# The retention output projection of a two-layer block: seven Strassen products in place of full-depth products

## What is computed

```python
att = sliding_window_attention(aq, ak, av, att_sinks)
ret = retention_chunkwise(rq, rk, rv)
ret = head_group_norm(ret, ret_gn_gain) * jax.nn.silu(rg)
merged = jax.nn.sigmoid(ga) * (att @ w_att_o) + jax.nn.sigmoid(gr) * (ret @ w_ret_o)
x = x + merged @ w_out
```

## Time and profile before

| | |
|---|---|
| runs | 2552.01, 2551.42, 2550.05 us (median 2551.42) |
| profiled execution | 2549.01 us, of which the span from first to last instruction is 2547.2 us |
| DVE busy | 1555.7 us, 61% |
| ACT busy | 1032.7 us, 41% |
| POOL busy | 1210.2 us, 48% |
| DMA | 46.3% of the 16 engines' span |

### The profile page before, as it was taken

How to read it: one execution, slowest core, us unless ns; L and a number is a source line. 1 busy time by engine, 2 the same in 40 slices (tenths; PEclk the granted TensorE clock), 3 DMA queues, 4 the chain that set the end, 5 groups by cost and what they waited for, 6 DMA issues and landing times. The chain is left out here.

```text
span 2547.2 us, 34818 instructions
## 1 busy us (share of the span) xinstructions
PE 2518.6 (99%) x12750; PEld 2100.7 (82%) x12750; DVE 1555.7 (61%) x2576; ACT 1032.7 (41%) x2097; POOL 1210.2 (48%) x970
## 2 busy tenths in 40 slices
PE   8999999999999999999999999999999999999998
PEld 7888888777888988888888878898889888888887
DVE  6455444675436545454599852248657666587789
ACT  5332333584224322232444552147646233254443
POOL 4587766354525767676212672314556444200205
PEclk9999999999999999999999999999999999999999
DMA  6565665705551233333753345548443333364434
GB/s 220 203 238 208 226 229 190 281 18 190 191 189 67 96 137 114 117 117 108 273 191 102 100 151 164 175 93 180 143 125 116 108 110 118 135 233 143 177 100 169
DMA packets 171158, 397.55 MB, mean 156 GB/s; under 512 B 22818, under 2 KB 43938, under 8 KB 167330
## 3 DMA queue, kind: packets, MB, share of 16 engines
q1 hardware_dynamic: 170988, 395.32, 46.3%
HBM read 282.69 MB, written 112.31 MB: 155 GB/s over the span
## 5 line engine op out<-in xcount | busy, mean ns | idle before, releaser
L2450 POOL TENSOR_TENSOR WL<-WRAW,WH 128x512 fp32r<-128x512 f32 (+1 forms) x150 | 250.1, 1668 | 360.3 <-ACT WH L1126 359.9
L876 PE MATMUL PS<-HH,WL 128*128 128x512 f32 (+1 forms) x976 | 367.6, 377 | 1.0 <-DVE HS L2016 1.0
L879 PE MATMUL PS<-HH,WH 128*128 128x512 f32 (+1 forms) x976 | 366.5, 375 | 0.0
L878 PE MATMUL PS<-HL,WH 128*128 128x512 f32 (+1 forms) x976 | 366.5, 375 | 0.0
L1652 DVE TENSOR_TENSOR WL<-TS,WH 128x512 fp32r<-128x512 f32 x228 | 230.5, 1016 | 174.3 <-ACT WH L1126 174.1
L944 PE MATMUL PS<-WH,DAL 128*128 128x512 f32 x756 | 294.7, 390 | 0.4 <-DVE WL L1959 0.4
L946 PE MATMUL PS<-WH,DAH 128*128 128x512 f32 x756 | 294.4, 389 | 0.0
L945 PE MATMUL PS<-WL,DAH 128*128 128x512 f32 x756 | 294.4, 389 | 0.0
L2642 POOL TENSOR_TENSOR X<-X,DV 128x512 f32<-128x512 f32 x56 | 90.9, 1646 | 349.2 <-DVE DV L2079 270.9
L876 PEld LDWEIGHTS PS<-HH,WL 128*128 128x128 f32 x976 | 183.8, 188 | 34.3 <-DVE HS L2016 1.3
L1126 ACT ACTIVATE WH<-TS 128x512 fp32r<-128x512 f32 x228 | 138.4, 621 | 180.6 <-POOL TS L2466 180.5
(11 more groups left out here) (359 smaller groups left out, 5880.1 us busy)
## 6 DMA issues: line engine op xcount, KB each, us to landing
WRAW<-in_u_f SPq DMA_DIRECT2D x56, 512.0 KB, 3.7
WRAW<-in_u_in SPq DMA_DIRECT2D x54, 512.0 KB, 4.1
WRAW<-scr_t SPq DMA_DIRECT2D x52, 512.0 KB, 3.7
scr_h<-HS SPq DMA_DIRECT2D x96, 256.0 KB, 2.3
WRAW<-in_u_gu SPq DMA_DIRECT2D x44, 512.0 KB, 3.6
scr_t<-TTa SPq DMA_DIRECT2D x19, 1024.0 KB, 4.8
WRAW<-in_u_out SPq DMA_DIRECT2D x24, 512.0 KB, 3.6
scr_x<-X SPq DMA_DIRECT2D x24, 512.0 KB, 5.0
```

The source lines that it names most:

```text
L876: e.matmul(PS[:, b, 0:wd], wl[:, blk(kk)], op_moving(q, kk, c0, wd, 0), start=(kk == 0), stop=False)
L878: e.matmul(PS[:, b, 0:wd], wh[:, blk(kk)], op_moving(q, kk, c0, wd, 1), start=False, stop=False)
L879: mm = e.matmul(PS[:, b, 0:wd], wh[:, blk(kk)], op_moving(q, kk, c0, wd, 0), start=False, stop=(kk == 3))
L2450: e.tensor_tensor(lo, raw, hi.bitcast(F32), ALU.subtract).then_inc(*c.inc("w_lo_p", i))
```

## The change

The retention's output projection becomes seven products P1, P2, P5, P6, P3, P7, P4 (in that order, `DORDER`), each of four groups m = 0 to 3 of 12 matmuls: 28 groups, 336 matmuls in place of 384. P2 is accumulated on the banks of P1, P3 on those of P5, P4 on those of P7, after ACT (P1, P5) or DVE (P7) has copied or drained them. "U" is P1+P6, "11" is P1+P2, "22" is first P5, then P5+U. The 16 merges go with the groups of P6, P3, P7 and P4; each has now three DVE operations: one with a bank as an operand (P6: U plus the bank; P3, P4: bank plus U; P7: bank plus "22"), then the multiplication by one gate and the addition of the other with both operands in SBUF. DVE makes the operand sums S1, S3, S2, S4 of the gated retention result (16 operations) and the low halves of S1 and S2, POOL the low halves of S4 and S3 and the four sums "22"+U; the low halves of A21 are not made any more. The weights come as 28 halves of 128x512, low halves alternately on DVE (`r0`) and POOL (`r1`), in place of eight whole units; four of the seven are sums that POOL makes ahead of time, so `NPAIR` goes from 27 to 31, and ten pairs in place of six are done in the first FFN, at m = 2, 4, ..., 20. The gate multiplications of the retention result go with the attention outputs as `GATE_AO` says, sixteen with ten, none after. The first group of the product with `w_out` waits for merge 7 (tile 7 of the first half), the second for merge 15 (tile 6 of the second half), which is the last.

```diff
-NPAIR = 27
+NPAIR = 31
...
-    units("u_ro", range(8))
+    for p in DORDER:
+        for m in (0, 2):
+            for x in range(2):
+                ROP[p, m + x] = len(ops)
+                ops.append((f"r{x}", len(order), n_pos()))
+            order.append(("r", (DPROD[p][1], m)))
...
-    LATE = [("P1", 1, 3 * g, 0) for g in range(1, 7)], [("P5", 1, 3 * g, 0) for g in range(1, 7)], [("P1", 1, 3 * g + 1, 0) for g in range(1, 7)]
-    N_RV, N_LATE = 3, 6
+    LATE = [[(p, 1, m + x, 0) for m in range(2, 22, 2)] for p, x in (("P1", 0), ("P5", 0), ("P1", 1))]
+    N_RV, N_LATE = 3, 10
...
     def t_weights(g):
-        return WU["u_dn"][2 * g:2 * g + 2] if g < FF1 // 2 else WU["u_f2"][2 * g - FF1:2 * g - FF1 + 2]
+        for name, t0 in (("u_f2", PAIRS_OF[2]), ("u_ro", T_RO), ("u_dn", 0)):
+            if g >= t0:
+                return WU[name][2 * (g - t0):2 * (g - t0) + 2]
...
-        return kind in ("B11", "B21") or i == PAIR[2, 0] + 6
+        return kind in ("B11", "B21", "r1") or i == PAIR[2, 0] + 6
...
-    RO2 = [(n, half) for half in range(2) for n in range(6)] + [(n, half) for half in range(2) for n in range(6, 8)]
+    GATE_AO = {1: 6, 3: 7, 4: 8, 6: 9, 7: 10, 9: 11, 11: 12, 12: 13, 14: 14, 15: 15}
+    RO_ON = {"P2": "P1", "P3": "P5", "P4": "P7"}
+    MERGED = ([(2 * m, 0) for m in range(4)] + [(2 * m + 1, 0) for m in range(4)]
+              + [(2 * m + 1, 1) for m in range(4)] + [(2 * m, 1) for m in range(4)])
+    MERGE_AT = ["P6", "P3", "P7", "P4"]
...
-        for n, half in RO2:
-            proj_t(("ro2", n, half), U["u_ro", n], half, RH, RL, low="rg_l")
+        for p in DORDER:
+            q = DPROD[p][0]
+            for m in range(4):
+                key, i, onto = ("roP", p, m), ROP[p, m], p in RO_ON
+                if onto:
+                    b = bk.again(key, ("roP", RO_ON[p], m))
+                    w.wait_ge(*bk.empty(key))
+                else:
+                    b = open_bank(key, p in RO_ON.values())
+                w.wait_ge(*lo_done(i))
+                wh, wl, hi, lo = half_slot(WH, i), half_slot(WL, i), ro_half(q, RH), ro_half(q, RL)
+                for kk in range(4):
+                    w.wait_ge(*ro_low(q, kk))
...
+                mm.then_inc(*bk.fill(key))
+                used(i, key)
+            for m in range(4 if p in RO_ON else 0):
+                bk.drop(("roP", p, m))
...
-            w.wait_ge(*c.at("mg_l", (7, tt // 4)))
+            w.wait_ge(*c.at("mg_l", (6 if tt // 4 else 7, tt // 4)))
...
+            if j >= 4 or half == 0:
+                w.wait_ge(*c.at("rg_m", i))
+                e.activation(RH[:, j, hs(half)], QK[:, j, hs(half)], ACT.Copy).then_inc(*c.inc("rg_h", (j, half)))
+            if i in GATE_AO:
+                feed(("ao", *AOG[GATE_AO[i]]))
...
+        for p in DORDER:
+            for m in range(4):
+                key = "roP", p, m
+                if p in ("P1", "P2", "P5"):
+                    w.wait_ge(*bk.full(key))
+                    e.activation(ro_sum({"P1": "U", "P2": "11", "P5": "22"}[p], m), PS[:, bk.at(key), :],
+                                 ACT.Copy).then_inc(*bk.free(key))
+                if p in ("P2", "P5", "P6"):
+                    ro_high({"P2": "S2", "P5": "S4", "P6": "S3"}[p], m)
+                if p in MERGE_AT:
+                    i = 4 * MERGE_AT.index(p) + m
+                    n, half = MERGED[i]
+                    w.wait_ge(*c.at("mg_a", i))
+                    if p == "P6":
+                        w.wait_ge(*ro_low("S2", 3))
+                        w.wait_ge(*ro_low("S4", 3))
+                    if p == "P3":
+                        w.wait_ge(*ro_low("S3", 3))
+                    e.activation(HH[:, n, hs(half)], MR[:, i % 2, :], ACT.Copy).then_inc(*c.inc("mg_h", (n, half)))
+                feed(key)
...
-            if i + N_TAIL < 16:
-                att_out(i + N_TAIL)
-                feed(("ao", *AOG[i + N_TAIL]))
-        for i, (n, half) in enumerate(RO2):
-            key = "ro2", n, half
-            w.wait_ge(*bk.full(key))
+            if i in GATE_AO:
+                att_out(GATE_AO[i])
+                feed(("ao", *AOG[GATE_AO[i]]))
...
+        def ro_sums(q, j):
+            left, right, sign = {"S1": ("A21", "A22", ALU.add), "S3": ("A11", "A21", ALU.subtract),
+                                 "S2": ("S1", "A11", ALU.subtract), "S4": ("A12", "S2", ALU.subtract)}[q]
+            if q == "S1":
...
+            e.tensor_tensor(ro_whole(q)[:, j, :], ro_whole(left)[:, j, :], ro_whole(right)[:, j, :], sign).then_inc(
+                *c.inc("s_ov", ("ro", q, j)))
...
+        def ro_lows(q, j):
+            w.wait_ge(*c.at("h_hi", ("ro", q, j)))
+            e.tensor_tensor(ro_half(q, RL)[:, j, :], ro_whole(q)[:, j, :], ro_half(q, RH)[:, j, :].bitcast(F32),
...
+        def merge(i):
+            n, half = MERGED[i]
+            p, m, mr = MERGE_AT[i // 4], i % 4, MR[:, i % 2, :]
+            key = "roP", p, m
+            if i >= 2:
+                w.wait_ge(*c.at("mg_l", MERGED[i - 2]))
+            if p == "P6":
...
+            elif p == "P7":
+                src = ro_sum("22", m)
+                w.wait_ge(*bk.full(key))
+                w.wait_ge(*c.at("s_op", ("ro", "22", m)))
+                e.tensor_tensor(src, PS[:, bk.at(key), :], src, ALU.add).then_inc(*bk.free(key))
+                w.wait_ge(*bk.out(key))
+            else:
+                src = mr
+                w.wait_ge(*bk.full(key))
+                w.wait_ge(*bk.out(("roP", "P6", m)))
+                e.tensor_tensor(mr, PS[:, bk.at(key), :], ro_sum("U", m), ALU.add).then_inc(*bk.free(key))
+                w.wait_ge(*bk.out(key))
             w.wait_ge(*c.at(f"lg{i % 2}", i))
             w.wait_ge(*c.at(f"lm{i % 2}", i))
-            if i >= 2:
-                w.wait_ge(*c.at("mg_l", RO2[i - 2]))
-            e.tensor_tensor(MR[:, i % 2, :], PS[:, bk.at(key), :], MG[:, i % 2, 0, :],
-                            ALU.mult).then_inc(*bk.free(key))
-            w.wait_ge(*bk.out(key))
-            e.tensor_tensor(MR[:, i % 2, :], MR[:, i % 2, :], MG[:, i % 2, 1, :],
-                            ALU.add).then_inc(*c.inc("mg_a", i))
-            feed(key)
+            e.tensor_tensor(mr, src, MG[:, i % 2, 0, :], ALU.mult).then_inc(*c.inc("s_ov", ("ro", "mg", i)))
+            w.wait_ge(*c.at("s_ov", ("ro", "mg", i)))
+            e.tensor_tensor(mr, mr, MG[:, i % 2, 1, :], ALU.add).then_inc(*c.inc("mg_a", i))
+
...
+        for j in range(4):
+            ro_sums("S1", j)
+        for p in DORDER:
+            for m in range(4):
+                key = "roP", p, m
+                if p == "P1":
+                    ro_lows("S1", m)
+                    ro_sums("S3", m)
+                    ro_sums("S2", m)
+                elif p == "P2":
+                    ro_lows("S2", m)
+                    ro_sums("S4", m)
+                elif p == "P6":
+                    w.wait_ge(*bk.full(key))
+                    w.wait_ge(*bk.out(("roP", "P1", m)))
+                    e.tensor_tensor(ro_sum("U", m), PS[:, bk.at(key), :], ro_sum("U", m), ALU.add).then_inc(*bk.free(key))
+                if p in MERGE_AT:
+                    merge(4 * MERGE_AT.index(p) + m)
+                feed(key)
...
+        def merged_low(i):
+            n, half = MERGED[i]
+            w.wait_ge(*c.at("mg_h", (n, half)))
+            e.tensor_tensor(HL[:, n, hs(half)], MR[:, i % 2, :], HH[:, n, hs(half)].bitcast(F32),
+                            ALU.subtract).then_inc(*c.inc("mg_l", (n, half)))
+
         for i in range(16):
             j, half = GATED[i]
+            if j < 4 and half:
+                if i in GATE_AO:
+                    feed(("ao", *AOG[GATE_AO[i]]))
+                continue
...
+        for p in DORDER:
+            for m in range(4):
+                key = "roP", p, m
+                if p in ("P5", "P6"):
+                    q = "S4" if p == "P5" else "S3"
+                    w.wait_ge(*c.at("h_hi", ("ro", q, m)))
+                    e.tensor_tensor(ro_half(q, RL)[:, m, :], ro_whole(q)[:, m, :], ro_half(q, RH)[:, m, :].bitcast(F32),
+                                    ALU.subtract).then_inc(*c.inc("s_op", ("ro", "lo", q, m)))
+                if p == "P3":
+                    w.wait_ge(*bk.out(("roP", "P5", m)))
+                    w.wait_ge(*bk.out(("roP", "P6", m)))
+                    e.tensor_tensor(ro_sum("22", m), ro_sum("22", m), ro_sum("U", m),
+                                    ALU.add).then_inc(*c.inc("s_op", ("ro", "22", m)))
+                if p in MERGE_AT:
+                    merged_low(4 * MERGE_AT.index(p) + m)
+                feed(key)
...
+            if name == "r":
+                kind, m = i
+                if kind[0] == "T":
+                    for t in range(T_RO + m, T_RO + m + 2):
+                        w.wait_ge(*c.at(f"ts{t_set(t)}", ("out", t)))
+                    src = bass.AP(scr_t.tensor, scr_t.offset + 2048 * P * (T_RO + m) + 512 * T_SLOT[kind],
```

(15 more changed lines are left out.)

## The result

| | before | after |
|---|---|---|
| median | 2551.51 us | 2581.39 us |
| lowest to highest of 4 runs | 2550.05 to 2552.01 | 2579.80 to 2582.28 |
| span of the profiled execution | 2547.2 us | 2578.9 us |

The ratio is 1.0117, with a 95% interval of 1.0100 to 1.0135: slower, as forecast, but 18.4 us beyond the 2563.0 forecast and outside of the range (2546 to 2569).

What follows compares the result with a forecast made beforehand. PE was taken to bound the kernel. Later start of w_out's second group +9.0, before P6 +1.0 and slow matmuls +1.6 gave +11.6 us on 2551.4: 2563.0 us, range 2546 to 2569.

Steps and rivals of the forecast that it cites:

- Matmuls removed: Retention's output projection on PE: 48 fewer matmuls at 0.2267 us save 10.9 us, before anything is given back.
- The walk: DVE's merges from P6 to P4 take 63.95 us, so w_out's second group starts 9.0 us later than now.
- DVE keeps pace: Rival, in the merges: POOL's and DVE's SBUF operations hardly meet, 8.4 us gained, 2543.0 us; chance 0.16.
- each waits for the whole of the other's operation: Rival, in DVE-POOL meetings: 0.24 us more in some 25 of them, 6 us, 2569 us; chance 0.10.
- the two share without gaps: Rival, in the merges: DVE and POOL work totals 56.1 us, 0.2 us gained, 2551.2 us; chance 0.15.
- Before P6: Gates to S2's low halves: the last low half of S1 comes 1 us late at P5, shifting the walk +1.0 us.
- PE after idle time: After 11.7 us idle before w_out's second group, eight matmuls take 0.2 us more each: +1.6 us, bounds 0 and 3.
- Weight sums: First FFN: four more pairs, 22 us of operations, fit in POOL's 119 us of idle time, so 0.
- My rival for it: Rival, in the first FFN: weight sums make POOL late with low halves, at most 5 us, 2568 us; chance 0.04.

Runs made afterwards that it cites:

- e4: Kernel before with only the sixteen gate multiplications interleaved with the ten attention outputs: 2550.0 us, ratio 1.0002.
- e13: e5 with sums S3 and S4 on 8 columns and RG loads cut to 32 of 512 columns from the fifth on: 2569.6 us, ratio 1.0080.
- e5: e1 plus DVE making all four low halves of S1 before adding S3, and of S2 before S4: 2576.8 us, ratio 1.0107.
- e1: Changed kernel with ACT copying P1's four banks to U between gate tiles 12 to 15: 2575.6 us, ratio 1.0106.
- e8: Kernel before with four added, unread weight-sum pairs, ten in the first FFN at m = 2, 4, ..., 20: 2553.9 us, ratio 1.0015.
- e9: e8 with the first FFN's ten pairs at m = 1, 3, ..., 19 instead: 2550.2 us, ratio 1.0001.
- e2: Changed kernel with each merge's multiplication and addition reading the bank, not their SBUF operand, sums left out: 2569.2 us, ratio 1.0080.
- e10: e5 with ACT's and w_out's orders changed, "11" merged from banks, "22" by DVE, S3/S4 by POOL, last weight pair as in e9: 2564.4 us, 1.0056.

## Why the prediction was wrong, step by step

**Matmuls removed, -10.9: right.** 12702 in place of 12750, and the spacing of the new products' matmuls is 0.2267 wherever PE has not stood.

**The walk, 63.95 us: right.** 66.2 measured. The mean of the 32 SBUF operations is (8.6 + 8.3 + 23.7) / 32 = 1.27 us, 1.26 in the walk. The units' waits for ACT are 4.9 us in three, 1.65 each in the walk. The last low half came 2.0 us behind DVE, 2.05 forecast. Of the 2.2 us too little, the waits for MG (3.0) make the most; I had taken 0 and bounded them by 2. The rival "DVE keeps pace" (a mean under 0.98) is refuted by these rows, and so are "each waits for the whole of the other's operation" (6 us more over 32 operations, a mean of 1.45) and "the two share without gaps" (56.1 us; POOL was idle for 18.9 us of 682 to 749).

**Before P6, +1.0: this step failed.** The chain started at 682.4, which is 11.7 us after the 670.7 that the forecast comes to. Two faults lie beside each other, and each alone makes the chain late:
- I followed the operands of P2 but not its bank. "The matmuls of P1 and P2 use tiles gated long before" is true; that P2 also waits for ACT's copy of P1, and what stands ahead of that copy in ACT's order, I did not write down. It made a stop of 9.4 us and 2.5 us of slow matmuls. The bound of 4 us for the early part knew of S1's low halves alone.
- I had DVE ready for its first merge step when PE had done P6's first group, and it was not. The gates end at 647.6 and not 642.6, though interleaved (e4: 648.4 without the rest of the change; e13: the loads of RG are 3.7 us of it). The last low half of S2 then came 25.0 us later, at 672.6, where I had allowed 25.9. Behind it stood one more sum and two weight halves, up to 680.0. My account before P6 has DVE's 24 sums and low halves and POOL's weight halves, but none of the weight halves that DVE makes itself. There were seven: 7.5 us and 4.3 us of waiting for ACT's high halves in the changed kernel, 10.1 us and 0.6 in e5. In all the front work took 32.4 us (32.3 in e5, 31.3 in e1).

DVE's weight halves in 648 to 680 us of the changed kernel, then the end of its front work:

```profile
L1735 DVE TENSOR_TENSOR WL<-WRAW,WH 128x512 fp32r<-128x512 f32 x7 | 7.5, 1072 | 4.3 <-ACT WH L1181 4.3
...
670.81 1.77 DVE L1999 TENSOR_TENSOR RL<-QK,RH 128x512 fp32r<-128x512 f32 x1
672.51 0.68 DVE L1994 TENSOR_TENSOR QK<-QK 128x512 f32<-128x512 f32 x1
673.16 1.73 DVE L1735 TENSOR_TENSOR WL<-WRAW,WH 128x512 fp32r<-128x512 f32 x1
678.60 1.36 DVE L1735 TENSOR_TENSOR WL<-WRAW,WH 128x512 fp32r<-128x512 f32 x1 [3.71 <-ACT WH L1181]
```

The last wait of 3.71 us may itself come from PE's stop (ACT's high half stands there behind copies of P5's banks), but in e1 and e5, without the stop, DVE is no earlier than 678.9 and 681.1. So e1, which undoes only the first fault, gained some 3 us by the ratios.

**PE after idle time, +1.6: mechanism right, too small.** I costed the slow matmuls of one stop. There were four stops in this stretch and one in the down projection, with 2.5 + 1.7 + 1.7 + 2.6 + 1.6 = 10.1 us of slow matmuls. The stops at P7 and P4 cost nothing more, as I had written, and their slow matmuls neither, since the last merge was later still. The 2.5 us behind the stop at P2 are in the late start of the chain; the 2.6 us behind the last stop and the 1.6 us in the down projection count in full. The stop ahead of w_out itself was 9.4 us, "some 10" in the forecast. That the granted clock reads 1.00 at the kernel's start does not stand in the earlier trace rows, which begin at 607 us; that row is in the last section.

The Trainium skill (TensorE: Matmul & The Clock Gate, Wait — 56ns, not 53.3ns?) gives 426.7 ns from start to start for 512 columns at 1.2 GHz. The 0.43 us in the timeline agree.

**Weight sums, 0: failed.** They cost 3.9 us by e8 (3.7 between e8 and e9), and the changed kernel shows a stop of the same kind (2.2 us at 1281.7, 0.4 before). I had weighed POOL's and PE's time and taken the change of steps for a gain. What counted was that the last of ten pairs now ends at m = 20, so that its store falls into a stretch in which the DMA engines are busy for 0.92 to 0.96 of the time. My rival for it had POOL's work as its mechanism, which e9 refutes.

**The sum again**, by what was measured at each place, against the 2563.0:

| step | forecast | measured | difference |
|---|---|---|---|
| start of the chain | 670.7 | 682.4 | +11.7 |
| length of the chain | 63.95 | 66.2 | +2.2 |
| low half behind it | 2.05 | 2.0 | 0 |
| slow matmuls at w_out | 1.6 | 2.6 | +1.0 |
| weight sums | 0 | 3.7 to 3.9 | +3.8 |
| sum | | | +18.7 |

The median is 18.4 us above the forecast. By the spans (31.7 us apart, where the medians are 29.9) 1.4 us more would have to be found. Counted from the end, the same matmul of PE lies 29.9 us later than before at 1712 us and 31.7 later from 1957 us on; the cause of that step is open.

## What to carry to other kernels

When a product is accumulated on a bank that another engine must read first, follow that reader in its own written order, as one follows operands; and when one late thing is found, ask who else would have been late at the same place, because taking it away gains only the difference (9.4 us of stop, some 3 us of time here).

When the time is counted that an engine needs ahead of a step, its part of the weight work belongs in the list: seven weight halves were missing here, 8 to 12 us with their waits.

Where both queues are full, each SBUF operation of POOL costs DVE 1.1 us (128x512), so POOL is no place to move DVE's SBUF work to; the operations that escape are those with an operand in PSUM (0.69 us beside a POOL that is busy for three quarters of the time in e2, 1.27 with both operands in SBUF). Hidden work has to be hidden on every resource: look where its last transfer falls, and at the DMA share of that window, not of the span.

## What the hardware showed that I had not expected

- Two engines in turn: with both queues full, four operations of DVE and four of POOL in SBUF took 6.8 us (1.70 us a pair), seen twice in e10. DVE's with a bank as operand stayed at 0.68 to 0.69 us.
- The granted clock was at 0.50 for 5 us behind a stop of 9.4 us, and the matmuls at 0.43 us from start to start showed the same behind stops of 2.2, 4.3 and 4.6 us. At the start of the kernel before, where matmuls have the same spacing, the column reads 1.00, so there it does not show the level; the spacing of the matmuls does:

```profile
8.10:15.00 6.90, 5.89 (x22) 4.96 (x23) 5.12 (x8) 5.44 (x10) 0.61 (x2) 1.00 1.02 417
```

- One store of 1 MB, issued 0.5 us ahead of three weight fetches in a stretch with the DMA engines 0.92 to 0.96 busy in any case, moved the weight fetch behind it by 3.8 us.
